# The root-mean-square factor of four feed-forward sublayers is multiplied into the first product's results instead of into its inputs

## The reference

```
x = x + 0.5 * _swiglu(_rms_norm(x, ffn1_norm[l]), ffn1_wi[l], ffn1_wo[l])
u = _rms_norm(x, mix_norm[l])
...                     # three mixers of u, gated and added: merged
x = x + merged @ w_out[l]
x = x + 0.5 * _swiglu(_rms_norm(x, ffn2_norm[l]), ffn2_wi[l], ffn2_wo[l])

def _rms_norm(x, gain):
    y = xf * lax.rsqrt(jnp.mean(xf * xf, axis=-1, keepdims=True) + EPS)
    return y * gain

def _swiglu(u, wi, wo):
    a, g = jnp.split(u @ wi, 2, axis=-1)
    return (jax.nn.silu(a) * g) @ wo
```

## Time and profile before

| | |
|---|---|
| median of 3 runs | 3130.94 us (3130.02 to 3133.44) |
| the profiled execution's own time | 3132.72 us |
| its span | 3131.0 us |
| busy | PE 89%, DVE 54%, ACT 37%, POOL 11% |
| mean granted clock of PE | 0.938 |
| M0.ffn0.in0 | about 1982 to 2048 |
| M0.ffn1.in0, M1.ffn0.in0, M1.ffn1.in0 | about 2454 to 2520, 2557 to 2622, 3028 to 3095 |

### The profile page before, as it was taken

How to read it: one execution, slowest core, us unless ns; L and a number is a source line. 1 busy time by engine, 2 the same in 40 slices (tenths; PEclk the granted TensorE clock), 3 DMA queues, 4 the chain that set the end, 5 groups by cost and what they waited for, 6 DMA issues and landing times.

```text
span 3131.0 us, 41693 instructions
## 1 busy us (share of the span) xinstructions
PE 2796.3 (89%) x16044; PEld 2360.5 (75%) x16044; DVE 1705.8 (54%) x2664; ACT 1151.0 (37%) x1542; POOL 335.8 (11%) x419
## 2 busy tenths in 40 slices
PE   2999999999999999999979999788578999956889
PEld 1888867756688886888765899788358998944889
DVE  6654646574673646757456555555344555543454
ACT  2222242254421224212235534544344444433443
POOL 3100041122200022000210101000001000000100
PEclk9999999899999999999999999898679999956999
DMA  5443516311362533545320355444014445500444
GB/s 206 164 152 107 181 65 201 115 31 48 108 204 71 178 111 108 194 135 174 107 81 1 122 182 182 146 155 143 1 66 149 159 160 188 175 1 14 148 148 155
DMA packets 64341, 394.03 MB, mean 126 GB/s; under 512 B 7280, under 2 KB 8784, under 8 KB 29136
## 3 DMA queue, kind: packets, MB, share of 16 engines
q1 hardware_dynamic: 41504, 309.97, 28.5%
q0 software_dynamic: 22160, 80.23, 8.4%
q10 hardware_dynamic: 544, 2.00, 0.2%
HBM read 391.12 MB, written 1.05 MB: 125 GB/s over the span
## 4 chain that ended last, share of the span: by engine, by line
PE 71%; issue 17%; DVE 7%; ACT 3%; POOL 1%; DMA 1%; ACTq 0%; POOLq 0%; DVEq 0%
PE banks L390 20%; PE banks L392 19%; PE banks L391 19%; PE banks L861 2%; PE banks L880 2%; DVE wlo L355 2%; ACT whi L347 2%; PE banks L870 2%; DVE squares L454 1%; PE banks L405 1%; PE banks L417 1%; PE banks L416 1%; PE banks L415 1%; PE banks L406 1%; PE banks L407 1%
## 5 line engine op out<-in xcount | busy, mean ns | idle before, releaser
L355 DVE TENSOR_TENSOR wlo<-raw,whi 128x2048 fp32r<-128x2048 f32 (+1 forms) x240 | 594.4, 2477 | 381.0 <-ACT whi L347 381.0
L390 PE MATMUL banks<-uhi,whi 128*128 128x512 f32 (+1 forms) x1648 | 603.5, 366 | 3.0 <-DVE wlo L355 3.0
L391 PE MATMUL banks<-ulo,whi 128*128 128x512 f32 (+1 forms) x1648 | 602.3, 365 | 0.0
L392 PE MATMUL banks<-uhi,wlo 128*128 128x512 f32 (+1 forms) x1648 | 602.2, 365 | 0.0
L347 ACT CAST whi<-raw 128x2048 fp32r<-128x2048 f32 (+1 forms) x240 | 487.8, 2032 | 225.2 <-PE banks L392 184.7
L390 PE MATMUL banks<-u2hi,whi 128*128 128x256 f32 x1312 | 377.1, 287 | 26.4 <-DVE wlo L1715 23.8
L391 PE MATMUL banks<-u2lo,whi 128*128 128x256 f32 x1312 | 374.5, 285 | 0.0
L392 PE MATMUL banks<-u2hi,wlo 128*128 128x256 f32 x1312 | 374.4, 285 | 0.0
L390 PEld LDWEIGHTS banks<-uhi,whi 128*128 128x128 f32 x1648 | 311.1, 189 | 59.1 <-DVE wlo L355 3.4
L392 PEld LDWEIGHTS banks<-uhi,wlo 128*128 128x128 f32 x1648 | 311.2, 189 | 55.1
L391 PEld LDWEIGHTS banks<-ulo,whi 128*128 128x128 f32 x1648 | 311.2, 189 | 54.9
(11 more groups left out here) (349 smaller groups left out, 4493.5 us busy)
## 6 DMA issues: line engine op xcount, KB each, us to landing
raw<-in_ffn_in SPq DMA_DIRECT2D x132, 1024.0 KB, 5.0
raw<-in_ffn_out SPq DMA_DIRECT2D x48, 1408.0 KB, 6.1
mod_slot<-in_w_mod POOLq DMA_DIRECT2D x128, 512.0 KB, 3.9
raw<-in_w_merge SPq DMA_DIRECT2D x32, 1024.0 KB, 4.9
raw<-in_w_in SPq DMA_DIRECT2D x26, 1024.0 KB, 4.8
raw<-in_na_qkv SPq DMA_DIRECT2D x12, 1024.0 KB, 4.9
mod_start<-in_w_mod POOLq DMA_DIRECT2D x16, 512.0 KB, 13.0
raw<-in_w_out SPq DMA_DIRECT2D x8, 1024.0 KB, 5.0
```

Of the source, the lines that this page charges most:

```text
L355: dve.tensor_tensor(wlo[u % 2][:, 0:n], raw[u % 2][:, 0:n], whi[u % 2][:, 0:n].bitcast(F32), ALU.subtract).then_inc(lo_done, 1)
L390: pe.matmul(out, w_hi, x_hi[:, k, 0:T], start=(n == 0), stop=False)
L391: pe.matmul(out, w_hi, x_lo[:, k, 0:T], start=False, stop=False)
L392: mm = pe.matmul(out, w_lo, x_hi[:, k, 0:T], start=False, stop=(n == len(chunks) - 1))
```

## The change

In the four feed-forward sublayers of the second block (norms 7, 9, 10 and 12; M0 and M1's mixers keep the old way) the inputs of the first product are h * gain, without the factor. They are made as `h` comes: by ACT and DVE inside the output product ahead (9, 10, 12), or out of the layer norm (7), where gain and shift of the layer norm are multiplied by the new gain into `vX1` and `vX0`. PE starts the first unit without the mean of the squares, and takes the mean (`means_pe`) behind the first unit. ACT makes rstd while PE works. DVE then multiplies both halves of each unit by rstd when it takes them out of PSUM; silu reads and writes SBUF, and the product of the two is one more DVE instruction. The small table `v2` is loaded at the start of the program by SP, and the other three of the second block behind the squares of norm 7.

```
@@ rstd_act @@
-        if s in TAKES:
+        if s in TAKES and s != 7:
             split_hi(act, TAKES[s].u0 + 1, early=True)
...
+    def folded_hi_act(act, s, cc):
+        l, name = FOLDED[s]
+        act.activation(u2hi[:, cc, 0:S], h[:, cc, 0:S], ACT.Identity, scale=vec2(l, name, cc))\
+            .then_inc(*ACT_.up(("u hi", s, cc)))
+
+    def folded_lo_dve(dve, s, cc):
+        l, name = FOLDED[s]
+        dve.wait_ge(*ACT_.at("u hi", s, cc))
+        dve.scalar_tensor_tensor(u2lo[:, cc, 0:S], h[:, cc, 0:S], vec2(l, name, cc),
+                                 u2hi[:, cc, 0:S].bitcast(F32), ALU.mult, ALU.subtract)\
+            .then_inc(*DVE_.up(("u", s, cc)))
+
+    def last_norm1_dve(dve, s):
...
+        split_lo(dve, TAKES[s + 1].u0 + 1, early=True)
...
+        dve.tensor_tensor(vX1[:], vS1[:, s, :, 0], gain, ALU.mult).then_inc(*DVE_.up())
+        dve.tensor_tensor(vX0[:], vS0[:, s, :, 0], gain, ALU.mult).then_inc(*DVE_.up(("vX", s)))
+        centre_dve(dve, s, S)
+        dve.wait_ge(*ACT_.at("rstd", s))
+        for cc in range(KC + 1):
+            if cc < KC:
...
+                dve.tensor_tensor(h[:, cc, 0:S], h[:, cc, 0:S], rstd[:, 0:S], ALU.mult)\
+                    .then_inc(*DVE_.up(("n", s, cc)))
+            if cc < KC // 2:
+                centre_chunk(dve, s, S, cc + KC // 2)
+            if cc:
+                k = cc - 1
+                dve.wait_ge(*ACT_.at("u hi", s + 1, k))
+                dve.tensor_scalar(h[:, k, 0:S], h[:, k, 0:S], vS1[:, s, k, 0:1], vS0[:, s, k, 0:1],
+                                  ALU.mult, ALU.add).then_inc(*DVE_.up(("h", s, k)))
+                dve.wait_ge(*DVE_.at("h", s, k))
+                folded_lo_dve(dve, s + 1, k)
+
+    def last_norm1_act(act, s):
+        split_hi(act, TAKES[s + 1].u0 + 1, early=True)
+        rstd_act(act, s, S, True)
+        act.wait_ge(*DVE_.at("vX", s))
+        for cc in range(KC):
+            act.wait_ge(*DVE_.at("n", s, cc))
+            act.activation(u2hi[:, cc, 0:S], h[:, cc, 0:S], ACT.Identity, scale=vX1[:, cc:cc + 1],
+                           bias=vX0[:, cc:cc + 1]).then_inc(*ACT_.up(("u hi", s + 1, cc)))
...
+    def folded_in_act(act, name, buf):
...
+            split_hi(act, u + 1, it)
+            act.wait_ge(f_scaled, plus(g + 1, 2, it))
+            act.activation(buf["a"][:, u % 2, 0:S], buf["a"][:, u % 2, 0:S], ACT.Silu).then_inc(f_silu, 1)
+            act.wait_ge(f_full, plus(g + 1, 2, it))
+            act.copy(buf["hi"][:, i, 0:S], buf["full"][:, u % 2, 0:S]).then_inc(f_hi, 1)
...
+    def folded_in_dve(dve, name, s, buf):
...
+            split_lo(dve, u + 1, it)
+            if u == ph.u0:
+                dve.wait_ge(*ACT_.at("rstd", s))
+            dve.wait_ge(product, plus(2 * u + 2, 4, it))
...
+            dve.tensor_tensor(buf["a"][:, u % 2, 0:S], banks[:, bank(u, 0), 0:S], rstd[:, 0:S], ALU.mult)\
+                .then_inc(f_scaled, 1)
+            dve.tensor_tensor(buf["full"][:, u % 2, 0:S], banks[:, bank(u, 1), 0:S], rstd[:, 0:S], ALU.mult)\
+                .then_inc(evicted, 1)
+            dve.wait_ge(evicted, plus(u + 1, 2, it))
+            dve.wait_ge(f_silu, plus(f + 1, 2, it))
+            dve.tensor_tensor(buf["full"][:, u % 2, 0:S], buf["a"][:, u % 2, 0:S], buf["full"][:, u % 2, 0:S],
+                              ALU.mult).then_inc(f_full, 1)
...
@@ ffn_in_pe @@
                 first_unit(pe, ph, s, x_hi, x_lo, T)
+                if s in FOLDED:
+                    means_pe(pe, s, S, None)
...
@@ out_act @@
             split_hi(act, ph.u0 + i + 1)
+            if s in FOLDED:
+                for cc in (2 * i, 2 * i + 1):
+                    act.wait_ge(*last_evicted(ph)(cc))
+                    folded_hi_act(act, s, cc)
...
@@ out_dve @@
             split_lo(dve, u + 1)
+            if s in FOLDED and i:
+                for cc in (2 * i - 2, 2 * i - 1):
+                    folded_lo_dve(dve, s, cc)
...
+        if s in FOLDED:
+            for cc in (KC - 2, KC - 1):
+                folded_lo_dve(dve, s, cc)
+            split_lo(dve, TAKES[s].u0 + 1, early=True)
```

More of the change, by code:

```diff
@@ L1792, in _ @@
             s = 7 + 3 * l
-            means_pe(pe, s, S, None)
             ffn_in_pe(pe, f"M{l}.ffn0.in0", s, S, u2hi, u2lo)
@@ L1826, in _ @@
         block1_ffn("act", act, "L1.ffn1", 5, S)
[L1827 to L1830 removed]
+        last_norm1_act(act, 6)
+        squares_act(act, 7, S, lambda cc: DVE_.at("h", 6, cc), range(KC))
+        for dst, src in ((k2, "const2"), (rows2, "rows2"), (positions, "positions")):
             act.dma_start(dst[:], A[src]).then_inc(block2_loaded, 16)
[L1832 removed]
         for l in range(2):
             s = 7 + 3 * l
[L1835 to L1838 removed]
+            rstd_act(act, s, S, False)
+            folded_in_act(act, f"M{l}.ffn0.in0", NARROW)
             out_act(act, f"M{l}.ffn0.out0", s + 1, S)
@@ L1890, in _ @@
             merge_dve(dve, l)
-            out_dve(dve, f"M{l}.wo", S, lambda cc, kind: 1.0, None)
-            norm2_dve(dve, s + 2, l, "ffn2_norm", u2hi, u2lo)
-            ffn_in_dve(dve, f"M{l}.ffn1.in0", S, NARROW)
-            out_dve(dve, f"M{l}.ffn1.out0", S, half_gate, None)
+            out_dve(dve, f"M{l}.wo", S, lambda cc, kind: 1.0, None, s + 2)
+            folded_in_dve(dve, f"M{l}.ffn1.in0", s + 2, NARROW)
+            out_dve(dve, f"M{l}.ffn1.out0", S, half_gate, None, s + 3 if l == 0 else None)
     @block.gpsimd
```

52 lines of the change are left out of this document (35 added, 17 removed).

## The result

| | before | after |
|---|---|---|
| median of 5 runs | 3130.02 us (3120.31 to 3133.44) | 3148.96 us (3144.72 to 3154.79) |
| ratio, 95% interval | | 1.0067 (1.0047 to 1.0087) |
| the profiled execution's own time, span | 3132.72, 3131.0 us | 3144.72, 3143.0 us |
| busy | PE 89%, DVE 54%, ACT 37% | PE 89%, DVE 55%, ACT 37% |

What follows compares the result with a forecast made beforehand. PE was taken to bound the kernel, with 71% of the chain. Handover gains of 15.35 us against losses of 12.8 + 0.6 made -2.0 us, from the median 3130.9 a forecast of 3129 us, range 3119 to 3142.

Steps and rivals of the forecast that it cites:

- handover s = 7: From the layer norm to DVE's first multiplication of unit 1 in M0.ffn0.in0: that multiplication 4.2 us earlier.
- handovers s = 9, 10, 12: From the output products ahead to the input products' first multiplication: 2.5, 4.8 and 3.85 us gained, net of slower output products.
- the loop, without the clock: Four input products: the longer DVE-ACT chain sets the pace at 6.05 us a unit, losing 3.2 each, 12.8 in all.
- lower clock in third units: Behind the layer norm (s = 7), PE may do the third unit at the lower clock: 1.6 us, 0.6 counted.
- rival 1: PE falls to 1.2 GHz at new waits, 1.7 us each, 14 in eight places: 3143 us; chance 0.10.
- What follows A(10) keeps its distance: Behind DVE's first multiplication of unit 10: the next output product starts no later relative to it, its weights split as before.
- The rest costs nothing: Loading v2 at the program's start, among SP's issues, and giving up its place behind the norm: no cost.
- never for PE's product: Sign expected in the input-product loop: DVE waits for ACT's cast, never for PE, with multiplications about 6.05 us apart.
- some 0.5 for the mean: In the handovers from output products: PE's mean of the squares, behind the first unit, takes some 0.5 us.
- the turns in M0.wo: Output product ahead of norm 9: additions 7.1 us apart, 1.58 more a turn, the last ending 4.7 later.
- rival 4: Silu's table load holds ACT for twice its 1.28 us, 5.1 more in four handovers: 3134 us; chance 0.03.
- Rival 2: Input-product loop: the chain is longer still, 6.3 us a unit, 7.7 more in all: 3137 us or more; chance 0.17.

Runs made afterwards that it cites:

- r1_after: The changed kernel run once more, unchanged: 3147.30 us, ratio 1.0062 to the kernel before.
- e4: The changed kernel with five more, unused PE matmuls behind the second unit of each of the four input products: 3139.62 us, ratio 1.0014 to the kernel before.
- e1: The kernel before with only the changed kernel's tile placement in SBUF, no instruction changed: 3139.65 us, ratio 1.0018.
- e3: The kernel before with only the four input-product loops done in the changed way (multiplying by rstd twice): 3147.95 us, ratio 1.0044.
- e8: The kernel before with weight casts and splits moved earlier in the input products, and casts in the output products ahead of norms 9, 10, 12: 3125.39 us, ratio 0.9968.
- e10: The kernel before with padding so that all tiles PE streams as data start 64 bytes past a multiple of 128: 3107.83 us, ratio 0.9920.
- e11: The kernel before with the changed kernel's tile placement and 64 unused bytes ahead of f2hi: 3137.44 us, ratio 1.0007 to the kernel before.

## Why the prediction was wrong

By its own terms, against the stage table (the sum goes from -2.0 to +16.9):

| term | forecast | measured |
|---|---|---|
| handover s = 7 | -4.2 | -4.5 |
| handovers s = 9, 10, 12 | -2.5, -4.8, -3.85 | -2.5, -2.9, -2.6 |
| the loop, without the clock | +12.8 | +16.5 |
| lower clock in third units | +0.6 | +6.0 |
| placement | 0 | +1.7 at the end, and 2.6 of the +5.2 below |
| the mixers' stretches, M0.ffn0.out0 and M1.ffn0.out0 in them | 0 | +5.2 |

- **The step that failed most is the last of the handover from the layer norm: PE "may do the third unit at the lower clock: 1.6, of which I count 0.6".** The mechanism was seen, but for s = 7 alone and at about a third of a chance. It happened in all four sublayers, in this execution and in that of r1_after. For the other three the text had rival 1, with its waits "about 1.6 us and apart by a whole unit", in M0.wo and in the first units. The waits in M0.wo were 1.1 and its clock stayed at 1.00 (in r1_after it fell at the start of M0.wo, as it does in the kernel before); the wait that mattered was ahead of the third unit, which I hadn't followed for s = 9, 10 and 12. Its length can be had from the forecast's own numbers: the third unit's split ends just as A(1) begins, at 12.3 behind the last addition, and PE is done with the second unit some 2 us sooner. e4 shows its price, 1.5 each.
- **"What follows A(10) keeps its distance" failed in the same way.** The weights come as before, but PE stands idle for some 1.7 ahead of them and not 1.2, and in two of the four output products its clock fell: 3.0 us, which no term and no rival had.
- **"The rest costs nothing: the load of v2 ... its place behind the norm is given up" failed altogether.** I had asked what the load of `v2` costs and not what its new place does to all that lies behind it. e1 prices the placement at 5.6 us, by declarations alone. In the stages of the changed kernel it is 1.7 in the last output product. M0.ffn0.out0 and M1.ffn0.out0, inside the mixers' stretches, took 2.8 more each, 1.3 of it placement (as in e1) and 1.5 the clock: 5.6, against the +5.2 of these stretches. The rest of them scatters: in kernels whose mixers are as before (e1, e3, e8, e10, e11) M0's stretch takes 377.3 to 379.9.
- **The loop was mis-sized.** That the longer chain sets the pace was right, and the chain was sized well: 3.76 from A to the split and 2.21 for the split, 5.97 in the mean, where 6.05 was forecast. But a turn is 6.12: another 0.15 passes in the mean, mostly in DVE's wait for PE's product; that it would wait "never for PE's product" failed. A(1) to A(2) is 6.30, not 5.83, for the same reason at full size: the third unit's weights come when A(1) comes, and PE needs its whole unit after them. 0.47 and seven times 0.07, less 0.03 in the last step, in four sublayers: 3.7.
- **The handover was mis-sized by PE's mean.** 12.3 was counted for s = 9 and 12 and 12.7 for s = 10; it was 13.5, 13.5 and 14.2 (the end of the last addition, 2451.54, to 2465.05 for s = 9). The "some 0.5 for the mean" is 1.4: six matmuls of 256 columns, the first at 2455.87 and the next weight product only at 2457.28, and ACT idles 1.17, 1.85 and 1.17 for them. The gain of s = 9 looks right by luck: the clock fell at the start of M0.wo in the profile before and not in the one after, which is worth 1.3.
- Right: the turns in M0.wo (7.1 forecast, 7.14), the handover of s = 7, the wide turns in M0.ffn1.out0 (8.6 forecast; 8.58 for the second), and silu's table load at its bare price. In the changed kernel's timeline of ACT, ahead of M0.ffn0.in0:

```profile
1979.09 1.28 ACT L792 ACT_TABLE_LOAD   x1
1980.38 0.42 ACT L792 ACTIVATE silu_a<-silu_a 128x256 f32<-128x256 f32 x1
```

 Silu starts 1.29 after the load and no idle stands ahead of the load, so rival 4 is not borne out. The Trainium skill ("ScalarE: Activation LUTs", What ACT_TABLE_LOAD costs) counts a further drain of about 1.38 us for each switch; this trace does not agree with it.

The misses add up: 5.4 (clock), 3.7 (loop), 3.1 (the last three handovers, in which the lucky 1.3 of M0.wo is contained), -0.3 (the first), 1.7 and 5.2 (the end, and the mixers' stretches) are 18.8, and with the -2.0 they make +16.8, against 16.9. That it closes says only that no stretch was left out, for all terms are from the same two profiled executions. Rival 1 was right in kind: six falls of the clock, 9.0 us, though not in the places that it named. Rival 2's 6.3 a unit was not reached. What the range did not allow for is that the clock, the placement and small misses in every term come together on the slow side.

## What to carry to other kernels

When a wait is taken away in front of an engine, follow the engine past it: here PE started earlier, ran through the two units whose weights were ready, and stood still later, ahead of the third, where the idle time also cost it its clock. When a step is added to a chain across two engines, look first at what else stands between the same two handovers; moving the independent weight cast and split ahead of the hi-cast gave 30 us, more than the whole change was to bring; the same order in the kernel before, with the casts in the output products moved too, gave 10. And a declaration that moves tiles is an edit of its own: time it alone, and compare the distance from matmul to matmul in a stretch whose instructions are unchanged.
